# The last four units of an output projection as two blocks of Strassen's seven products, their weight sums made on GpSimd

## The chip, the cores and the metric

The kernel runs on one core of one Trainium2 chip. A core has TensorE (PE, matrix products), VectorE (DVE), ScalarE (ACT), GpSimd (POOL) and SyncE (SP), which here only issues the loads of weights. The metric is the device time of one execution in microseconds (us), the median of several runs. Everything is float32.

## The reference

One inference step of a two-layer hybrid encoder, for 256 prompt frames and 64 frames of a running stream (T = 320 frames together), 1024 channels wide. What matters here, cut:

```
h = rms(x, norm_mix);  p = h @ w_in                      # columns for four head groups of 256 channels
y_a = head_rms(lru(p), on[:G])  * gelu(lru_g)            # mixT rows 0, 1
y_b = head_rms(attention(p), on[G:2G])                   # mixT rows 2, 3
y_c = head_rms(retention(p), on[2G:3G]) * silu(r_g)      # mixT rows 4, 5
y_d = head_rms(mlstm(p), on[3G:])       * sigmoid(m_o)   # mixT rows 6, 7
x = x + concat([y_a, y_b, y_c, y_d]) @ w_out             # (320, 1024) @ (1024, 1024): the stage in question
gu = rms(x, norm_ffn) @ w_gu
x = x + (silu(gu[..., :2816]) * gu[..., 2816:]) @ w_down
```

The states of every group (latents, LRU, retention, mLSTM) are outputs too.

## The kernel before

Activations are held transposed: xT, hT and mixT are tiles of 128 channels by 320 frames, eight of each. Weights stream through a ring of five slots of 1 MB (chunks); SP loads chunk g when the use that frees chunk g-5 is done (the table LAST_USE, wait_used). Chunks o0 to o3 hold w_out, 256 output columns each, so a chunk serves two units of 128 output channels; f0 to f21 hold w_gu, then come those of w_down.

Nearly all of the large products except the output projection are already formed in blocks of Strassen's seven products: a block of two by two tiles takes seven products of half the frames (160 columns, HT) instead of eight. POOL makes three sums of the weights into spare memory and one in place (`a21 += a22`); DVE makes four sums of the activations, and puts the products together behind PE. Products 3, 5, 6 and 7 wait for POOL's sums (the semaphore "mixed"), and products 4 to 7 for those of the activations. The output projection is formed plainly: `project(n, ks)` adds the products of unit n for the tiles ks of mixT into bank n of PSUM, 320 columns each. Its order on PE follows the order in which the groups become ready: tiles 6, 7 (mLSTM), 2, 3 (attention, "mix1"), 4, 5 (retention, "mix2"), 0, 1 (LRU, "mix0"). Between them stand `pair_out` and `pair_mean` of the retention and the two mean products am0 and am1 of the LRU group, on which mix0 hangs: am0 and am1 go to ACT (two functions each), and DVE multiplies their results into mixT.

The order on each engine is written out by hand. An engine runs its instructions in that order, and `step` makes it wait for each result before the next. On POOL, the order of the stretch is: the retention states' stores, a wait until all stores have landed, the LRU stores (lru_conv, lru_h; single elements), a wait until they have landed ("a_out"), in layer 0 the loads of the next layer's latents, and then `mix_weights(l, i)` for f1, f2 and so on, the second of which waits for DVE's "h_sums". DVE waits for a_out before it makes h_sums.

Behind the projection, DVE adds each unit to xT ("x_new"), ACT squares it and multiplies it by the gain, DVE adds the squares up, PE sums them over the channels (ms2) in the middle of the first hidden units (fa0, fb0), and ACT makes rstd of that.

The part of `project` and its calls, as PE has them between the retention and the hidden units:

```
pair_mean(1, l)
project(4, (6, 7, 2, 3))
need(pe, "h_sq", l, 1)
for t in range(2):   # am0, am1
    ...
project(5, (6, 7, 2, 3))
for n in range(6):
    project(n, (4, 5))
for n in range(6):
    project(n, (0, 1))
for n in range(6, KT):
    project(n, (6, 7, 2, 3, 4, 5, 0, 1))
```

## Time and profile before

| | |
|---|---|
| three runs | 901.88, 902.30, 902.46 us; median 902.3 |
| profiled execution | 902.27 us, its span 900.40 us |
| PE, busy | 893.2 us, 99% |
| DVE, busy | 510.7 us, 57% |
| POOL, busy | 512.6 us, 57% |
| ACT, busy | 226.7 us, 25% |
| share of the chain of waits on PE | 86% |
| the output projection's line (L1295) in that chain | 7.7% |

The span runs from the first instruction to the last; the time of the execution has a little around it. A busy share is the share of the span in which the engine had an instruction under way. The chain of waits follows back from the last instruction, at each step to what released it. In timelines each row has the start in us, the duration in us, the engine, the line of the kernel, the operation, what it writes and reads, and in brackets how long the engine was idle before it and what ended that.

### The profile page before, as it was taken

How to read it: one execution, taken by the hardware profiler on the slowest of the kernel's cores; microseconds unless marked ns; L12 is line 12 of the kernel's file. 1: busy time of each engine (PE TensorE's matmuls, PEld its weight loads, DVE VectorE, ACT ScalarE, POOL GpSimd, SP SyncE). 2: the span in 40 equal slices, each digit the busy share in tenths (PEclk: the TensorE clock that was granted, in tenths of full speed). 3: DMA queues.
4: the chain of work that ended last, by engine and by line, in shares of the span. 5: the costliest groups of instructions: out<-in, count | busy, mean ns of one | idle time of the engine just before them, and what ended most of it. 6: DMA issues, size and time to landing. Idle time of an engine off the chain costs nothing.

```text
span 900.4 us, 15552 instructions
## 1 busy us (share of the span) xinstructions
PE 893.2 (99%) x5984; PEld 813.1 (90%) x5984; DVE 510.7 (57%) x1001; ACT 226.7 (25%) x497; POOL 512.6 (57%) x514
## 2 busy tenths in 40 slices
PE   8999999999999999999999999999999999999998
PEld 7997878778999999999979878877799999999998
DVE  6677857735656565522366776575565656573221
ACT  3334356531000000101133334573300000000001
POOL 6851474316866666666457344912297666666770
PEclk9999999999999999999999999999999999999999
DMA  9969321238545553333444774130844555434421
GB/s 277 279 107 110 104 92 52 54 82 240 141 141 142 140 140 129 130 129 130 128 134 144 31 151 98 48 97 5 191 138 140 140 140 141 141 130 130 151 83 36
DMA packets 159091, 112.92 MB, mean 125 GB/s; under 512 B 9829, under 2 KB 156682, under 8 KB 158890
## 3 DMA queue, kind: packets, MB, share of 16 engines
q1 hardware_dynamic: 154402, 104.44, 40.0%
q0 software_dynamic: 3984, 6.74, 7.3%
q8 instruction: 48, 0.79, 0.4%
q10 hardware_dynamic: 632, 0.75, 0.3%
q14 instruction: 25, 0.20, 0.1%
HBM read 108.33 MB, written 2.27 MB: 123 GB/s over the span
## 4 chain that ended last, share of the span: by engine, by line
PE 86%; DVE 7%; ACT 3%; DMA 1%; issue 1%; POOL 0%; SPq 0%; DVEq 0%; ACTq 0%; POOLq 0%
PE ps L1336 54%; PE ps L1295 8%; PE ps L871 7%; PE ps L905 3%; PE ps L891 2%; PE ps L1354 2%; PE ps L1005 1%; PE ps L1229 1%; PE ps L1093 1%; DMA out_s_mn<-sst 1%; DMA arena<-in_x_sample 1%; PE ps L1221 1%; PE ps L1062 1%; DVE work L2117 1%; PE ps L979 0%
## 5 line engine op out<-in xcount | busy, mean ns | idle before, releaser
L680 POOL TENSOR_TENSOR work<-ring 128x512 f32<-128x512 f32 (+1 forms) x66 | 81.8, 1240 | 153.9 <-issue 111.1
L1336 PE MATMUL ps<-mixT,ring 128*128 128x160 f32 x672 | 105.0, 299 | 0.0
L1336 PE MATMUL ps<-hT,work 128*128 128x160 f32 x672 | 98.5, 299 | 0.0
L1336 PE MATMUL ps<-hT,ring 128*128 128x160 f32 x672 | 98.1, 299 | 0.0
L1336 PEld LDWEIGHTS ps<-mixT,ring 128*128 128x128 f32 x672 | 95.8, 190 | 0.0
L1336 PEld LDWEIGHTS ps<-hT,ring 128*128 128x128 f32 x672 | 93.7, 190 | 0.3
L1336 PEld LDWEIGHTS ps<-hT,work 128*128 128x128 f32 x672 | 93.7, 190 | 0.0
L681 POOL TENSOR_TENSOR ring<-ring 128x512 f32<-128x512 f32 (+1 forms) x66 | 82.6, 1251 | 5.2
L682 POOL TENSOR_TENSOR work<-ring 128x512 f32<-128x512 f32 (+1 forms) x66 | 82.1, 1244 | 5.2
L1803 ACT ACTIVATE arena<-ps 128x160 f32<-128x160 f32 x42 | 12.8, 304 | 286.9 <-PE ps L1336 286.9
L683 POOL TENSOR_TENSOR work<-ring,work 128x512 f32<-128x512 f32 (+1 forms) x66 | 81.9, 1240 | 5.2
L871 PE MATMUL ps<-hT,ring 128*128 128x320 f32 x256 | 72.9, 437 | 0.0
L1295 PE MATMUL ps<-mixT,ring 128*128 128x320 f32 x256 | 70.4, 433 | 0.0
L2403 DVE TENSOR_TENSOR arena<-arena,ps 128x160 f32<-128x160 f32 x8 | 2.6, 322 | 118.6 <-ACT arena L1821 118.6
L1295 PEld LDWEIGHTS ps<-mixT,ring 128*128 128x128 f32 x256 | 48.5, 190 | 20.1
L871 PEld LDWEIGHTS ps<-hT,ring 128*128 128x128 f32 x256 | 47.4, 190 | 18.9 <-issue 1.0
L1336 PE MATMUL ps<-work,ring 128*128 128x160 f32 x352 | 55.6, 299 | 0.0
L1336 PE MATMUL ps<-mixT,work 128*128 128x160 f32 x336 | 52.5, 299 | 0.0
L1336 PE MATMUL ps<-arena,work 128*128 128x160 f32 x352 | 51.7, 299 | 0.0
L1336 PEld LDWEIGHTS ps<-work,ring 128*128 128x128 f32 x352 | 50.4, 190 | 0.0
L1336 PEld LDWEIGHTS ps<-arena,work 128*128 128x128 f32 x352 | 49.1, 190 | 0.0
L1336 PE MATMUL ps<-arena,ring 128*128 128x160 f32 x330 | 48.7, 299 | 0.0
(455 smaller groups left out, 1624.0 us busy)
## 6 DMA issues: line engine op xcount, KB each, us to landing
ring<-in_w_gu SPq DMA_DIRECT2D x88, 512.0 KB, 5.2
ring<-in_w_in SPq DMA_DIRECT2D x44, 512.0 KB, 6.4
ring<-in_w_down SPq DMA_DIRECT2D x32, 512.0 KB, 4.5
ring<-in_w_out SPq DMA_DIRECT2D x16, 512.0 KB, 4.6
ring<-in_w_down SPq DMA_DIRECT2D x16, 384.0 KB, 3.5
cst<-in_consts POOLq DMA_DIRECT2D x1, 1664.0 KB, 11.6
ring<-in_w_in SPq DMA_DIRECT2D x2, 640.0 KB, 5.8
arena<-r POOLq DMA_DIRECT2D x8, 160.0 KB, 18.0
```

Of the source, the lines that this page charges most:

```text
L680: step(tt(s3, a11, a21, ALU.subtract))
L681: step(tt(a21, a21, a22, ALU.add))
L682: step(tt(s2, a21, a11, ALU.subtract))
L683: step(tt(s4, a12, s2, ALU.subtract), "mixed")
L871: ins = mm(bank(use, 0, T, m), w[:, k, c:c + m], right[:, k, 0:T], start=(k == 0), stop=(k == KT - 1))
L891: ins = mm(bank(use, at * HT, HT), left, right, start=(opens and k == 0), stop=(k == KT // 2 - 1), skip_group_check=True)
L905: ins = mm(bank(use, at * HT, HT), left(k), right(k), start=(opens and k == 0), stop=(k == KT // 2 - 1), skip_group_check=True)
L1005: ins = mm(flat[a * HD:(a + 1) * HD, base:base + n], left(a), right(a), start=start, stop=stop, skip_group_check=True)
L1295: ins = mm(bank(u, 0, T), w[:, k, (n % 2) * P:(n % 2 + 1) * P], mixT[:, k, :], start=(k == 6), stop=(k == 1), skip_group_check=True)
L1336: ins = mm(bank(use, at * HT, HT), left, right(k), start=(opens and k == 0 and at == 0), stop=(closes and k == n - 1), skip_group_check=True)
L1354: return mm(bank(use, 0, T), w[:, k, q * P:(q + 1) * P], xg[:, k, :], start=(k == 0), stop=(k == KT - 1))
L1803: step(A(p1c[:, j % 2, :], bank(f"fa{j}", 0, HT), ACT.Copy), "p1_copied")
```

## The change

The units 4 to 7 (chunks o2 and o3) are no longer formed by `project` but as two blocks of seven products, `out_product`, with k running over the four pairs of tiles of mixT. Products 1, 2 and, for o2, 3 are begun early, for the tiles whose groups are ready. POOL makes the weights' sums of o2 and o3 (`out_weights`), in its order behind the retention stores and ahead of the LRU stores; `mix_weights(l, 0)` moves ahead of the wait for the LRU stores. DVE makes four sums of mixT ("mix_sums") after mix0, and puts the blocks together (`out_pair`); ACT copies the first product out of PSUM and squares units 4 to 7 in pairs. In layer 0 the loads of the latents wait for the last product of both blocks, as their memory holds sums.

```diff
@@ bank uses, per layer
-    u += [(f"o{n}", (n,)) for n in range(KT)]
-    u += [("ms2", (2,)), ("fa0", (0,)), ("fb0", (1,))]
+    u += [(f"o{n}", (n,)) for n in range(4)]
+    u += [("p2a", (4,)), ("p2c", (5,)), ("p3a", (6,)), ("p3c", (7,)), ("p2b", (0,)), ("p3b", (1,))]
+    u += [("ms2", (3,)), ("fa0", (0,)), ("fb0", (2,))]
@@ slots fall free
-LAST_USE.update({f"o{i}": f"o{2 * i + 1}" for i in range(4)})
+LAST_USE.update({f"o{i}": f"p{i}c" if i in OUTS else f"o{2 * i + 1}" for i in range(4)})
@@ POOL
+            def out_weights(l, i):
+                name = f"o{OUTS[i]}"
+                w, _ = quarters(name, l)
+                s2, s3, s4 = osum[i]
                 wait_chunk(pool, name, l)
                 a11, a12, a21, a22 = w[:, :, 0, 0, :], w[:, :, 1, 0, :], w[:, :, 0, 1, :], w[:, :, 1, 1, :]
                 tt = nc.gpsimd.tensor_tensor
+                step(tt(s3, a11, a21, ALU.subtract))
+                step(tt(a21, a21, a22, ALU.add))
+                step(tt(s2, a21, a11, ALU.subtract))
+                step(tt(s4, a12, s2, ALU.subtract), "mixed")
...
                         pool.wait_ge(sem("out_done"), 16 * nout[0])
                         now_made(pool, "state_out")
+                for i in range(len(OUTS)):
+                    out_weights(l, i)
                 need(pool, "lru_x_in", l, 1)
...
+                mix_weights(l, 0)
                 pool.wait_ge(sem("out_done"), 16 * nout[0])
                 now_made(pool, "a_out")
                 if l + 1 < DEPTH:
-                    wait_filled(pool, "kv2", l)
+                    for p in OUTS:
+                        wait_filled(pool, f"p{p}c", l)
                     load_latents(l + 1)
-                for i in range(MIXES):
+                for i in range(1, MIXES):
                     mix_weights(l, i)
@@ PE, after pair_mean(1, l); out_product waits for the weights' sums for 3, 5, 6, 7, for mix_sums for 4 to 7
-                project(4, (6, 7, 2, 3))
+                early, late, every = (3, 1), (2,), (3, 1, 2, 0)
+                out_product(2, 1, early, opens=True)
+                out_product(2, 2, early)
+                out_product(2, 3, early, opens=True)
                 need(pe, "h_sq", l, 1)
                 for t in range(2):
                     claim(pe, f"am{t}", l)
                     fill(mm(bank(f"am{t}", 0, AW), C("headmean"), an[:, t, :], start=True, stop=True), f"am{t}")
-                project(5, (6, 7, 2, 3))
-                for n in range(6):
+                for n in range(4):
                     project(n, (4, 5))
-                for n in range(6):
+                for which in (1, 2, 3):
+                    out_product(2, which, late)
+                out_product(3, 1, early + late, opens=True)
+                out_product(3, 2, early + late)
+                for n in range(4):
                     project(n, (0, 1))
-                for n in range(6, KT):
-                    project(n, (6, 7, 2, 3, 4, 5, 0, 1))
+                for which in (1, 2, 3):
+                    out_product(2, which, (0,))
+                for which in (1, 2):
+                    out_product(3, which, (0,))
+                out_product(2, 6, every, closes=True)
+                out_product(2, 5, every, opens=True)
+                out_product(2, 7, every, closes=True)
+                out_product(2, 4, every, closes=True)
+                out_product(3, 6, every, closes=True)
+                out_product(3, 5, every, opens=True)
+                out_product(3, 7, every, closes=True)
+                out_product(3, 3, every, opens=True)
+                out_product(3, 4, every, closes=True)
@@ ACT
-                squares(l, 1)
+                squares(l, 1, range(4))
+                for p in OUTS:
+                    need(act, "x_new", l, 2 * KT, 2 * p)
+                    wait_filled(act, f"p{p}a", l)
+                    step(A(pair_p1, bank(f"p{p}a", 0, HT), ACT.Copy), "p1_copied")
+                    squares(l, 1, range(2 * p, 2 * p + 2))
@@ DVE, after mix0
+                step(v.tensor_tensor(msum[0], m_at(0, 1), m_at(0, 0), ALU.subtract), "mix_sums")
+                step(v.tensor_tensor(msum[2], m_at(1, 1), msum[0], ALU.subtract), "mix_sums")
+                step(v.tensor_tensor(msum[1], m_at(1, 1), m_at(0, 1), ALU.subtract), "mix_sums")
+                step(v.tensor_tensor(msum[3], m_at(1, 0), msum[2], ALU.subtract), "mix_sums")
...
+                    need(dve, "p1_copied", l, P1S, NPAIR + OUTS.index(p) + 1)
+                    step(v.tensor_tensor(pair_u2, pair_p1, bank(a, HT, HT), ALU.add))
+                    step(v.tensor_tensor(x11, x11, pair_p1, ALU.add))
+                    step(v.tensor_tensor(x11, x11, bank(a, 2 * HT, HT), ALU.add), bank_read=(a, l))
+                    wait_filled(dve, b_, l)
...
+                    step(v.tensor_tensor(x22, x22, pair_u34[:, HT:T], ALU.add))
+                    step(v.tensor_tensor(x22, x22, bank(b_, 0, HT), ALU.add), bank_read=(b_, l))
+                    step(v.tensor_tensor(mid, mid, pair_u34, ALU.add))
+                    wait_filled(dve, c, l)
+                    step(v.tensor_tensor(mid, mid, bank(c, 0, T), ALU.add), "x_new")
+                    now_read(dve, c)
+                    now_made(dve, "x_new")
...
-                for n in range(KT):
+                for n in range(4):
                     wait_filled(dve, f"o{n}", l)
                     step(v.tensor_tensor(xT[:, n, :], xT[:, n, :], bank(f"o{n}", 0, T), ALU.add), "x_new")
                     now_read(dve, f"o{n}")
                     if n > 1:
...
+                        squares_so_far(n)
+                for p in OUTS:
+                    squares_so_far(2 * p)
+                    out_pair(p)
+                    squares_so_far(2 * p + 1)
```

## Rows read from the trace of the kernel before

**Rows 1.** The page: busy us (share) and instructions of PE; granted clock in 40 slices.
```profile
PE 893.2 (99%) x5984; PEld 813.1 (90%) x5984; DVE 510.7 (57%) x1001; ACT 226.7 (25%) x497; POOL 512.6 (57%) x514
...
PEclk9999999999999999999999999999999999999999
```
**Rows 2.** Waits of PE from 16 us on, longest first: us in total, times, longest.
```profile
PE ps L1229 <- ACT arena L1678: 0.8, 1, 0.8
```
**Rows 3.** The chain of waits, 160 to 215 us: start, us, engine, line, instructions.
```profile
174.16 2.15 PE ps L1295 x8
176.31 1.09 PE ps L1317 x4
177.40 23.69 PE ps L1295 x88
201.09 2.69 PE ps L1354 x10
```
**Rows 4.** The chain of waits in layer 1.
```profile
617.61 23.69 PE ps L1295 x88
```
**Rows 5.** The chain of waits: a block of 28 products, 160 columns.
```profile
475.23 7.61 PE ps L905 x56
```
**Rows 6.** Timeline of POOL, 155 to 222 us.
```profile
174.20 1.52 POOL L691 DMA_DIRECT2D out_p_lru_conv<-arena  x2 [1.77 <-DMA out_s_ret<-sst]
...
178.30 1.07 POOL L691 DMA_DIRECT2D out_s_lru_h<-arena  x2
196.56 0.76 POOL L698 DMA_DIRECT2D pckv<-in_cache_mla_ckv  x1 [17.19 <-DMA out_s_lru_h<-arena]
...
201.38 1.26 POOL L680 TENSOR_TENSOR work<-ring 128x512 f32<-128x512 f32 x1 [2.78 <-DMA ring<-in_w_gu]
202.72 1.40 POOL L681 TENSOR_TENSOR ring<-ring 128x512 f32<-128x512 f32 x1
```
**Rows 7.** Timeline of DVE, 155 to 222 us; 179.62 completes mix0.
```profile
173.96 0.83 DVE L2317 TENSOR_TENSOR arena<-arena 128x646 f32<-128x646 f32 x1
174.83 1.15 DVE L2319 SCALAR_TENSOR_TENSOR arena<-arena,cols 128x323 f32<-128x323 f32 x2
176.01 0.82 DVE L2322 TENSOR_TENSOR mixT<-work 128x640 f32<-128x640 f32 x1
...
179.62 0.23 DVE L2326 TENSOR_TENSOR mixT<-arena 128x64 f32<-128x64 f32 x1
...
201.20 0.49 DVE L2330 TENSOR_TENSOR xT<-xT,ps 128x320 f32<-128x320 f32 x1 [3.18 <-PE ps L1295]
```
**Rows 8.** Timelines where DVE and POOL meet; L2388's ns, shortest/median/longest.
```profile
527.60 2.02 DVE L2156 TENSOR_TENSOR arena<-arena 128x1792 f32<-128x1792 f32 x1
...
528.40 2.36 POOL L661 TENSOR_TENSOR pckv<-ring 128x512 f32<-128x512 f32 x1 [6.78 <-DMA out_s_mm<-mro]
...
201.83 1.15 DVE L2334 TENSOR_TENSOR hT<-hT 128x320 f32<-128x320 f32 x1
...
L2388 DVE TENSOR_TENSOR work<-arena,work x22: 324/1312/1318, 230.3 to 815.3; 128x160 f32<-128x160 f32 x22
```
**Rows 9.** Timeline of ACT, the last unit's square and gain.
```profile
201.78 0.47 ACT L1521 ACTIVATE hT<-xT 128x320 f32<-128x320 f32 x1 [3.24 <-DVE xT L2330]
202.28 0.56 ACT L1523 ACTIVATE work<-xT,cols 128x320 f32<-128x320 f32 x1
```
**Rows 10.** Busy time by stretch; the last columns are granted clock, DMA share, GB/s.
```profile
190.00:197.00 7.00, 7.00 (x28) 4.94 (x27) 3.45 (x8) 4.10 (x8) 0.44 (x1) 1.00 0.38 29
197.00:202.00 5.00, 5.00 (x20) 3.50 (x19) 1.53 (x4) 1.25 (x3) 2.22 (x4) 1.00 1.03 287
```
**Rows 11.** The same view at the end of the span.
```profile
895.00:900.00 5.00, 2.25 (x17) 1.74 (x15) 0.75 (x2) 0.76 (x2) 0.00 (x0) 0.97 0.23 66
```
**Rows 12.** Timeline of PE at both ends of the span.
```profile
1.07 4.99 PE L824 MATMUL ps<-work 128*128 128x128 f32 x24 [1.07 <-DVE work L1836]
...
897.23 0.44 PE L1414 MATMUL ps<-cst,xT 128*128 128x128 f32 x2 [0.41 <-DVE xT L2427]
```

More of the change, by code:

```diff
@@ L64 @@
 NPAIR = len(PAIRS)
+OUTS = (2, 3)
 MIXES = FT - 1 + 3 * NQ
-MADE = NPAIR + MIXES
-P1S = NPAIR + FT - 1 + NQ
+MADE = NPAIR + len(OUTS) + MIXES
+P1S = NPAIR + len(OUTS) + FT - 1 + NQ
 MSLOTS = 3
@@ L345, in build @@
         xgm = mixT
+        low = MSLOTS * 3 * 512 + KT * T
+        msum = [x.rearrange("p (k n) -> p k n", n=HT) for x in
+                (work[:, low:low + 4 * HT], work[:, low + 4 * HT:low + 8 * HT], work[:, low + 8 * HT:low + 12 * HT],
+                 arena[:, 2 * 326:2 * 326 + 4 * HT])]
+        pT1 = ytm_at + 640
+        osum = [[x.rearrange("p (k n) -> p k n", n=P) for x in three] for three in
+                ((pT0[:, 0:512], pT0[:, 512:1024], wkvb[:, :]),
+                 (work[:, pT1:pT1 + 512], work[:, pT1 + 512:pT1 + 1024], pckv[:, :, :].rearrange("p a n -> p (a n)")))]
         hp = mixT[:, :, :].rearrange("p k n -> p (k n)").rearrange("p (s k n) -> p s k n", s=4, k=4)
@@ L664, in pair_weights @@
                 step(tt(s4, a12, s2, ALU.subtract), "mixed")
+            def out_weights(l, i):
+                name = f"o{OUTS[i]}"
+                w, _ = quarters(name, l)
+                s2, s3, s4 = osum[i]
+                wait_chunk(pool, name, l)
+                a11, a12, a21, a22 = w[:, :, 0, 0, :], w[:, :, 1, 0, :], w[:, :, 0, 1, :], w[:, :, 1, 1, :]
+                tt = nc.gpsimd.tensor_tensor
+                step(tt(s3, a11, a21, ALU.subtract))
+                step(tt(a21, a21, a22, ALU.add))
+                step(tt(s2, a21, a11, ALU.subtract))
+                step(tt(s4, a12, s2, ALU.subtract), "mixed")
             def mix_weights(l, i):
@@ L1312, in _, with out_product @@
                 pair_mean(1, l)
-                project(4, (6, 7, 2, 3))
+                def out_product(p, which, ks, opens=False, closes=False):
+                    i = OUTS.index(p)
+                    use = f"p{p}" + {1: "a", 2: "a", 6: "a", 5: "b", 7: "b", 3: "c", 4: "c"}[which]
+                    if opens:
+                        claim(pe, use, l)
+                    wait_chunk(pe, f"o{p}", l)
+                    if which in (3, 5, 6, 7):
+                        need(pe, "mixed", l, MADE, NPAIR + i + 1)
+                    if which in (4, 5, 6, 7):
+                        need(pe, "mix_sums", l, 4)
+                    w, _ = quarters(f"o{p}", l)
+                    at = {1: 0, 2: 2, 6: 1, 5: 0, 7: 1, 3: 0, 4: 1}[which]
+                    for k in ks:
+                        need(pe, f"mix{k}", l, 1)
+                        left = {1: w[:, k, 0, 0, :], 2: w[:, k, 1, 0, :], 3: osum[i][2][:, k, :],
+                                4: w[:, k, 1, 1, :], 5: w[:, k, 0, 1, :], 6: osum[i][0][:, k, :],
+                                7: osum[i][1][:, k, :]}[which]
+                        right = {1: mixT[:, 2 * k, 0:HT], 2: mixT[:, 2 * k + 1, 0:HT], 3: mixT[:, 2 * k + 1, HT:T],
+                                 4: msum[3][:, k, :], 5: msum[0][:, k, :], 6: msum[2][:, k, :], 7: msum[1][:, k, :]}[which]
+                        ins = mm(bank(use, at * HT, HT), left, right, start=(opens and k == ks[0]), stop=(k == 0),
+                                 skip_group_check=True)
+                    if closes:
+                        fill(ins, use)
+                early, late, every = (3, 1), (2,), (3, 1, 2, 0)
+                out_product(2, 1, early, opens=True)
+                out_product(2, 2, early)
+                out_product(2, 3, early, opens=True)
                 need(pe, "h_sq", l, 1)
@@ L1330, in product @@
                     if p in (3, 5, 6, 7):
-                        need(pe, "mixed", l, MADE, NPAIR + i + 1)
+                        need(pe, "mixed", l, MADE, NPAIR + len(OUTS) + i + 1)
                     for k in range(n):
@@ L2363, in gate_up @@
                     p1 = p1c[:, j % 2, :]
-                    need(dve, "p1_copied", l, P1S, NPAIR + j)
+                    need(dve, "p1_copied", l, P1S, NPAIR + len(OUTS) + j)
                     step(v.tensor_tensor(u2, p1, bank(fa, HT, HT), ALU.add))
```

17 lines of the change are left out of this document (13 added, 4 removed).

## Prediction

> **What bounds the kernel now.** I read the busy shares first: PE is busy for 893.2 of 900.4 us [rows 1]. The list of waits on PE says the same from the other side: after the start its longest wait is 0.8 us [rows 2]. So every microsecond of product saved in the output projection can reach the end, and so can every microsecond that PE is made to wait. The chain of waits then gives the projection as an unbroken run on PE: pair_mean(1) to 174.16, four products, the two sums am0 and am1, 44 products to 201.09, then the first hidden units [rows 3]. Layer 1 repeats it 440.2 us later, with the same 23.69 us for the 44 [rows 4], so I work out layer 0 and double it. Last come the timelines of POOL, DVE and ACT around that run, for what the new steps must wait on.
>
> The profiled execution took 902.27 us: a span of 900.40 and 1.87 around it. The median of the three runs is 902.3, so the sum needs no correction.
>
> **Products, -2.0 us a layer.** A product 320 columns wide takes 23.69/44 = 0.538 us of PE [rows 3]; one of 160 columns takes 7.61/28 = 0.272 us (each is two instructions) [rows 5]. Removed are units 4 to 7, 32 x 0.538 = 17.23 us; added are 56 x 0.272 = 15.22 us. That is -2.01 us a layer and -4.0 us in all, the most that this change can bring.
>
> **The wait for the sums of o2, +5.5 us a layer.** After pair_mean(1) the new order on PE is products 1 and 2 of o2 for k = 3 and 1, four at 0.272 us, so at 174.16 + 1.09 = 175.25 it stands at product 3, which needs s4, the last of the four sums of o2 on POOL. These sums stand behind POOL's wait for the retention stores, in program order: POOL has issued the last of them at 172.43 and goes on only when it has landed, 1.77 us later, at about 174.15 [rows 6]. Ahead of these stores POOL mostly waits too, but the sums are queued behind and can't use it. A sum of 128x512 takes 1.27 us and the next begins 1.34 after it (201.38, 202.72 in layer 0) [rows 6], so s4 would be there at 174.15 + 3 x 1.34 + 1.27 = 179.5, and PE would wait 4.25 us. That is the lower bound.
>
> DVE disturbs them. From 173.96 to 176.83 it has four operations whose two operands are both in SBUF (646, 323, 323 and 640 columns) [rows 7], and where such operations meet POOL's the two take turns. A POOL sum that began at 528.40 during a DVE operation that ended at 529.62 ended at 530.76, 1.14 us after it; one that began at 202.72 ended at 204.12, 1.14 us after DVE's end at 202.98 [rows 6, 8]. In turn DVE's 160-column additions take 1.31 us beside POOL's (the median; the shortest, 0.32) [rows 8]. In turns, from 173.96 on: DVE to 174.79, POOL to 175.93, DVE to 176.27, POOL to 177.41, DVE to 177.75, POOL to 178.89, DVE to 179.56, POOL to 180.70 (DVE's own part is its columns at 0.96 a ns: at 202.64 POOL ended and DVE 0.34 us later for 320 columns). PE goes on at about 180.8 and has waited 5.5 us. I take 5.5, with 4.25 as the lower end and 6 as the upper.
>
> What is queued behind this wait on PE is am0 and am1. ACT and DVE then make mix0 of them: 3.54 us from the start of am0 to mix0 now [rows 3, 7]. am0 would start at 181.3, and with the sums of o3 on POOL beside DVE's four multiplications mix0 comes at about 186.7. PE asks for it after am (182.4), eight products of units 0 to 3 on mixT 4 and 5 (4.3) and nine small ones (2.4), at 189.2: covered by 2.5 us. It is covered now by 6.2 us (186.0 against 179.85). The four new mix_sums on DVE, 0.82 us each as the multiplication of the same 640 columns [rows 7], end at 190.2; PE wants them at 194.9. The sums of o3 end at 186.2 and are wanted later still. Without the wait, PE would be through with the projection at 199.1; with it, at 204.6.
>
> **Behind the projection, +1.0 us a layer.** Now one addition (0.49), a square and a gain on ACT (0.47, 0.56) and an addition (0.49) stand between the last unit and ms2, and PE covers them with five products (2.69 us) [rows 3, 7, 9]. In the new order units 6 and 7 are finished together, ACT's copy of p1 for o3 stands behind the squares and gains of units 4 and 5, and DVE does eight additions per pair. Counted from p2c (5.4 us ahead of the end): 0.6 for x_new, 2.1 for ACT's four, 0.3 for the copy, 2.8 for seven additions, 0.5 for the last, then square 6 and the addition to hT, about 1.1, plus four hand-overs of 0.1: the sum of squares is ready some 2.9 to 3.0 us after the end of the projection, not 2.69. That is +0.3 with POOL idle. But POOL forms the sums of f1 in this stretch, and four of these additions read SBUF alone; each pays up to 0.98 us [rows 8].
>
> When f1 arrives is open. Its slot falls free with unit 1, 20 products behind am (177.40 + 10.8 = 188.2), and POOL starts on it at 201.38; the transfers move only 29 GB/s from 190 to 197 and 287 after that, and the LRU stores, issued from 174.20 to 179.4, are waited for until 196.56 [rows 6, 10]. The new order issues these stores at 186.2 to 191.4 and f1 at 191.5, so if the stores hold the loads, f1 comes at 208 to 211; if not, at about 197. Early, it collides with the additions above. Late, its sums collide with h_ready (four operations of 640 columns, 0.82 us each alone), and a_out, which now also waits for these sums, comes at 214 to 217, where DVE wants it from about 213. In both cases I get 0.3 to 2.5 us and take 1.0. The latents are loaded later, after p3c; they are needed only at the end of the layer.
>
> **The clock, +1.3 us a layer.** The granted clock is full in every slice of the page [rows 1], with PE never idle for long; the last stretch, in which PE's last instruction starts at 897.23 and takes 0.44, shows 0.97: it fell to the lower level (1.2 GHz from 2.4) within the 2.8 us left [rows 11, 12]. A wait of 5.5 us is longer than anything that PE sees now, so I expect a fall in it. The first 24 instructions of the warm-up, 128 columns, take 4.99 us, 0.208 each [rows 12], where 160 columns take 0.136 later [rows 5]: half the speed. So a spell at the lower level lasted some 5 us here and would cost 2.5 us. The bounds are 0 and 2.5; part of a spell passes within the wait, so I take 1.3.
>
> The Trainium skill ("TensorE: Matmul & The Clock Gate", "What's actually happening") says that the throttled state is the default and activity releases it, so an idle array falls back. That a fall happens in mid-kernel no run here shows. By this rule the term stays; without it the sum would end 2.6 us lower.
>
> Another of its pages ("Perfetto Trace Analysis", the notes on GpSimd's profile boundary) has it that POOL's shown spans are unreliable and should be taken from start to start. With 1.27 us a sum the wait would be 0.3 us shorter than with the 1.34 that I took from the starts.
>
> **The sum.** -2.0 + 5.5 + 1.0 + 1.3 = +5.8 us a layer, +11.6 in all: 902.3 + 11.6 = 913.9 us.
>
> **Rivals.**
> *The clock holds.* The wait is there but PE stays at the upper level. For it: no fall is seen between the start and the end. 902.3 + 2 x 4.5 = 911.3 us.
> *No turns between POOL and DVE.* DVE's operations leave POOL alone; the wait is 4.25 us, the slip 0.3, the clock costs little (0 to 1): 902.3 + 2 x (-2.0 + 4.25 + 0.3 + 0.3) = 908.0 us. Against it stand the pairs of rows above.
> *f1 late.* The stores hold the loads longer than now; product 3 of f1 waits for POOL, and a_out holds the h_sums: 1.5 to 3 us a layer more, 917 to 920 us.
> *The sums are in time: faster.* If s4 of o2 is there when PE asks, only -2.0 and +0.3 a layer remain: 898.9 us. It decides at 177.0: s4 must come by then for the layer to be no slower, that is, POOL must start at 171.6 at the latest. What would allow it is that the wait for the stores isn't what holds POOL from 172.43 to 174.20. The trace names the landing of out_s_ret as releaser [rows 6], and even a start at 172.43 is too late.
> *Nothing changes*: only if gain and wait happened to cancel, s4 at 177.0.
>
> **Chances.** Forecast, with a fall of the clock in at least one layer: 0.50. Clock holds: 0.22. No turns: 0.08. f1 late: 0.12. In time: 0.06. Cancel: 0.02. A measurement of this kernel can tell about 0.2% (1.8 us) from no change; hence faster 0.06, same 0.02, slower 0.92. The range: the low ends of wait and slip without the clock give 908, the high ends with it 919; I set 908.5 to 918.0, which leaves out the fastest cases and part of f1 late.
>
> **What would show it.** PE idle ahead of the third product of o2 in both layers, released by POOL's fourth sum: 5.5 us (right), under 2 us (the wait was wrong). POOL's four sums spread over 6.5 us, not 5.4 (the turns). A granted clock under 1.00 in the 10 us behind the wait, with 160-column products at about 0.54 us. 56 products in 15.2 us. mix0 never waited for. Five products of f0 and then a gap of 0.3 to 2.5 us ahead of ms2, or a gap in f1. The prediction is wrong if POOL's sums of o2 start ahead of the retention stores, or if PE's wait is there but filled by work that the order lets pass.

## The result

The changed kernel takes 924.75 us (median of four runs, 923.31 to 926.25), the kernel before 902.38 (901.88 to 902.80): a ratio of 1.0247, 95% interval 1.0235 to 1.0259, so 22.4 us slower. The forecast was +11.6 us, with a range that ended at 918.0: the direction was right, the size half of what came, and the time lies outside the range.

The profiled execution took 926.25 us, its span 924.4. The page, to be laid beside [rows 1]: busy us of the engines, and the granted clock in 40 slices.

```profile
PE 900.9 (97%) x6080; PEld 826.4 (89%) x6080; DVE 538.3 (58%) x1033; ACT 228.0 (25%) x501; POOL 536.2 (58%) x530
...
PEclk9999999898999999999999999998999999999999
```

PE is busy 7.7 us longer than before, though the new order holds 4 us less of products, and its clock is no longer full in three slices. The rest is waiting. The waits of PE from 16 us on, where before had none over 0.8 us [rows 2] (us in total, times, longest):

```profile
PE ps L1359 <- POOL wkvb L687: 9.6, 2, 4.8
PE ps L1359 <- issue: 3.4, 1, 3.4
PE ps L1418 <- DVE hT L2409: 3.3, 2, 2.1
PE ps L1404 <- DVE hT L2444: 1.2, 1, 1.2
```

The first is product 3 of o2 waiting for POOL's s4, in both layers; the second a pause put down to no releaser, in layer 0; the third the sum of the squares (ms2); the fourth a product of f1, in layer 1. The timeline of PE has them in order, layer 0 (the line of [rows 3] in which the 44 products ran without a gap):

```profile
173.58 1.25 PE L1359 MATMUL ps<-mixT,ring 128*128 128x160 f32 x8
179.63 1.40 PE L1359 MATMUL ps<-mixT,wkvb 128*128 128x160 f32 x4 [4.80 <-POOL wkvb L687]
180.83 2.36 PE L1371 MATMUL ps<-arena,cst 128*128 128x323 f32 x4
182.98 4.96 PE L1322 MATMUL ps<-mixT,ring 128*128 128x320 f32 x16
...
201.32 0.98 PE L1359 MATMUL ps<-work,ring 128*128 128x160 f32 x6
205.66 1.09 PE L1359 MATMUL ps<-work,ring 128*128 128x160 f32 x2 [3.36 <-issue]
206.54 2.34 PE L1359 MATMUL ps<-work 128*128 128x160 f32 x8
...
217.12 1.65 PE L1418 MATMUL ps<-hT,cst 128*128 128x320 f32 x4 [2.15 <-DVE hT L2409]
218.57 7.54 PE L1422 MATMUL ps<-work,ring 128*128 128x320 f32 x22
```

Layer 1 has the first wait again, and a longer stretch of slow rows behind it:

```profile
635.22 1.40 PE L1359 MATMUL ps<-mixT,wkvb 128*128 128x160 f32 x4 [4.80 <-POOL wkvb L687]
636.42 2.36 PE L1371 MATMUL ps<-arena,cst 128*128 128x323 f32 x4
638.58 5.84 PE L1322 MATMUL ps<-mixT,ring 128*128 128x320 f32 x16
```

The timeline of the kernel before has this for am0 and am1:

```profile
176.15 1.25 PE L1317 MATMUL ps<-arena,cst 128*128 128x323 f32 x4
```

Four 323-column instructions (am0, am1) take 2.36 us behind the first wait and 1.25 in the kernel before; eight of 160 columns take 1.25 at 173.58 and 2.34 at 206.54. That is the lower clock. The same stretches by window (the last three columns are granted clock, DMA share, GB/s):

```profile
175.00:183.00 8.00, 3.37 (x9) 2.59 (x10) 4.95 (x4) 1.16 (x3) 7.61 (x6) 0.63 0.01 2
...
197.00:204.00 7.00, 5.30 (x39) 5.05 (x38) 0.96 (x3) 0.30 (x1) 0.00 (x0) 1.00 0.45 31
204.00:211.00 7.00, 5.31 (x19) 5.18 (x20) 3.10 (x7) 2.24 (x5) 0.00 (x0) 0.53 0.66 118
211.00:217.00 6.00, 3.98 (x19) 2.83 (x17) 4.93 (x9) 1.02 (x3) 4.26 (x4) 0.98 1.14 303
217.00:221.00 4.00, 3.88 (x9) 2.54 (x10) 1.03 (x3) 3.25 (x6) 3.27 (x4) 0.64 1.20 293
```

The clock fell three times in layer 0 (in the wait for s4, in the pause, and 1.0 us after the wait for ms2) and once in layer 1, in the wait for s4. The DMA row at 197 to 204 moves 31 GB/s where before had 287 from 197 to 202 [rows 10]. POOL's timeline shows what moved with it:

```profile
173.35 1.27 POOL L684 TENSOR_TENSOR arena<-ring 128x512 f32<-128x512 f32 x1 [1.35 <-DMA out_s_ret<-sst]
174.70 1.73 POOL L685 TENSOR_TENSOR ring<-ring 128x512 f32<-128x512 f32 x1
...
177.98 1.39 POOL L687 TENSOR_TENSOR wkvb<-ring,arena 128x512 f32<-128x512 f32 x1
...
185.38 1.55 POOL L714 DMA_DIRECT2D out_p_lru_conv<-arena  x2 [0.29 <-POOL pckv L687]
...
212.50 1.26 POOL L703 TENSOR_TENSOR work<-ring 128x512 f32<-128x512 f32 x1 [21.89 <-DMA ring<-in_w_gu]
```

The LRU stores go out 11.2 us later than in [rows 6] (185.38 against 174.20), and f1 is there 11.1 us later (212.50 against 201.38). DVE has a pause of its own in this stretch, between two additions of the first block; its operand from PE was complete at 199.3:

```profile
206.28 0.49 DVE L2421 TENSOR_TENSOR pair_t<-ps,pair_t 128x320 f32<-128x320 f32 x1 [7.59 <-remote]
```

The profiled executions differ by 926.25 - 902.27 = 24.0 us. The four falls of the clock, each the slow rows less the same groups at the full clock (1.25 us for four instructions of 323 columns, 4.47 for sixteen of 320, 0.71 for four of 160), cost 2.3, 3.1 and 1.9 us in layer 0 and 3.2 in layer 1, together 10.4 (or 10.6 by PE's busy time, 900.9 us against 890.3 in e7_tail_reordered below, which has the same 6080 instructions and in its profile a clock that never fell). Products -4.0, wait for s4 +9.6, the pause +3.4, the waits for ms2 and for h_ready +4.5 and the clock +10.4 make +23.9. That it closes so well is partly an offset of two errors of about 1 us: by busy time the seven products gave back only 2.9 us (890.3 against 893.2), and PE's idle time grew by 16.3 us (23.5 against 7.2), not by the 17.5 of these waits.

### The profile page after: what moved, and what is told of

It reads as the page before. It is cut to its first block, busy times and chain, and to the rows that moved or that the text cites. A ratio compares the mean times of both kernels' runs of the same rounds, so it can differ in the third digit from the quotient of the medians.

```text
span 924.4 us, 15855 instructions
## 1 busy us (share of the span) xinstructions
PE 900.9 (97%) x6080; PEld 826.4 (89%) x6080; DVE 538.3 (58%) x1033; ACT 228.0 (25%) x501; POOL 536.2 (58%) x530
## 4 chain that ended last, share of the span: by engine, by line
PE 82%; DVE 7%; ACT 4%; DMA 2%; POOL 2%; issue 2%; another core or an unknown queue 1%; SPq 0%; DVEq 0%; ACTq 0%; POOLq 0%
PE ps L1404 52%; PE ps L932 7%; PE ps L898 6%; PE ps L918 2%; PE ps L1322 2%; PE ps L1120 1%; PE ps L1359 1%; PE ps L1089 1%; PE ps L1152 1%; PE ps L1422 1%; DVE hT L2444 1%; DMA out_s_mn<-sst 1%; PE ps L1248 1%; DMA arena<-in_x_sample 1%
## 5 line engine op out<-in xcount | busy, mean ns | idle before, releaser
L1404 PEld LDWEIGHTS ps<-mixT,ring 128*128 128x128 f32 x672 | 95.8, 190 | 0.0
L1404 PEld LDWEIGHTS ps<-mixT,work 128*128 128x128 f32 x336 | 47.9, 190 | 0.0
L1404 PEld LDWEIGHTS ps<-arena,ring 128*128 128x128 f32 x330 | 46.1, 190 | 0.0
```

The costliest lines, as they stand in the source:

```text
L1404: ins = mm(bank(use, at * HT, HT), left, right(k), start=(opens and k == 0 and at == 0), stop=(closes and k == n - 1), skip_group_check=True)
```

## The experiments

All were timed beside the kernel before (901.7 to 902.1 us in the five groups of runs). Each time is a median, each ratio one to the kernel before on the same chip, with its 95% interval.

### e1_third_product_last: the wait for the sums taken away

```diff
-                out_product(2, 3, early, opens=True)
...
-                for which in (1, 2, 3):
+                for which in (1, 2):
...
+                out_product(2, 3, every, opens=True)
                 out_product(2, 4, every, closes=True)
```

> The changed kernel with one move on PE: product 3 of o2 is formed as a whole right ahead of its product 4 instead of early, so nothing on PE asks for POOL's sums before 190 us. Theory S (the wait for s4 of o2 and the clock that it costs are nearly all of the loss; the rest follows it): -2.0 us of products and +0.3 a layer remain, 899 us. Theory W (the LRU stores, issued at 185 to 191 instead of 174 to 179, hold all DMA until 17 us after the last one, so loads and instruction fetches come late): the wait of 4.8 us goes, but f1 still lands at about 212 and PE then waits for its sums for about 7 us a layer, with a fall of the clock: 914 to 920 us.

Measured: 920.4 us (914.1 to 921.1), ratio 1.019 (1.0157 to 1.0224). The wait for s4 is gone and only 4.4 us with it (the profiled execution, at 914.1 us, is 6 us quicker than the other three, so its trace shows the mildest case). The time is about what theory W said; its mechanism, some 7 us a layer of waiting for f1's sums, isn't there (1.2 us in all). Something else took the place of the wait for s4, on PE:

```profile
PE ps L1322 <- DVE mixT L2395: 6.8, 2, 4.3
```

and on DVE, which makes mix2 between POOL's sums:

```profile
174.37 2.04 DVE L2392 SCALAR_TENSOR_TENSOR arena<-arena,cols 128x323 f32<-128x323 f32 x2
176.44 1.77 DVE L2395 TENSOR_TENSOR mixT<-work 128x640 f32<-128x640 f32 x1
```

In [rows 7] the same two lines take 1.15 and 0.82 us and end at 176.83. With POOL's sums beside them they end at 178.21, and product 3 no longer stands ahead as work for PE. The sums at this place cost a wait either way: for themselves, or for what they hold up.

The Trainium skill ("SBUF — State Buffer", "Who interferes with whom") says that a DVE instruction with both inputs in SBUF contends with a GpSimd instruction that reads SBUF, and that one with at most one SBUF input, outside the two-port modes, doesn't. The traces agree on both halves: 1.77 against 0.82 us here, while the addition that reads PSUM (L2428 of the changed kernel, at 215.50 us) takes 0.49 us beside POOL's sums as without them.

### e2_no_lru_stores: the changed kernel without the LRU stores

Its edit leaves the eight `out(...)` calls of lru_conv and lru_h in each layer out, so these states aren't written.

> The changed kernel without the stores of the LRU states (lru_conv and lru_h of both layers are left out of the outputs); all else as changed. Theory W: f1 lands at about 200 in layer 0, the pause of PE in the middle of a product (3.4 us) and of DVE (7.6 us) go; the wait for s4 (4.8) with its clock (about 3.3) stays: 915 to 918 us. Theory S: the late stores are no cause, 924 to 925 us.

Measured: 918.2 us (914.7 to 919.1), ratio 1.0185 (1.0168 to 1.0202), 6.6 us less than the changed kernel and about what theory W gave. The pause of PE and that of DVE are gone, the two waits of 4.8 us for s4 stand. The DMA queues from 182 to 209 us, first of the changed kernel, in which not one block of the queue "instruction" falls in these 27 us:

```profile
DMA packets 1283, 0.53 MB, mean 20 GB/s; under 512 B 264, under 2 KB 1283, under 8 KB 1283
...
q1 hardware_dynamic: 1027, 0.52, 22.2%
q0 software_dynamic: 256, 0.01, 1.9%
```

and then of e2:

```profile
DMA packets 7661, 3.89 MB, mean 144 GB/s; under 512 B 112, under 2 KB 7659, under 8 KB 7659
...
q8 instruction: 1, 0.02, 0.3%
q14 instruction: 1, 0.01, 0.1%
```

The 256 small packets of q0 are the LRU stores, 8 KB by the sizes of their eight issues. In the changed kernel the loads of weights on q1, issued from 192.57, move at most 72 GB/s in any microsecond up to 206, and 251 or more only from 209; in e2 they run at 220 to 346 GB/s from 193.5 to 200. So the stores slow them. But the recorded packets of q0 all lie between 186 and 192, before the slow stretch; what holds the queues after that, the trace doesn't show.

### e3_before_late_stores: only the stores late, in the kernel before

```diff
+                wait_filled(pool, "o0", l)
                 need(pool, "lru_x_in", l, 1)
```

> The kernel before, with one wait added on POOL: the LRU stores are issued when unit 0 of the projection is done (about 187.2 us in layer 0), 13 us later than before and 2 us later than in the changed kernel. No Strassen in the projection, no sums. Theory W: the stores hold f1 until about 210; f1's sums end at about 219 and PE waits for them about 6 us a layer, plus the clock and perhaps a pause for instructions: 918 to 926 us. Theory S or any theory in which the late stores only delay a_out (which would come at about 209.6, ahead of DVE's need at 210.2): 902 to 903 us.

Measured: 929.5 us (928.6 to 931.7), ratio 1.031 (1.0295 to 1.0326): with no other edit, stores that go out 13 us later cost 27.8 us, more than theory W gave them. POOL's row:

```profile
214.50 0.76 POOL L698 DMA_DIRECT2D pckv<-in_cache_mla_ckv  x1 [22.22 <-DMA out_s_lru_h<-arena]
```

and PE's waits:

```profile
PE ps L1337 <- issue: 17.7, 2, 9.4
PE ps L1337 <- DMA ring<-in_w_gu: 3.4, 2, 2.9
```

The stores land 22.2 us after the last was issued (24.4 in layer 1), where before it was 17.2 [rows 6], and PE waits for the load of f1 itself. But the 9.4 us are no pause: PE goes on at 222.88, 0.1 us after POOL's fourth sum of f1 has ended (221.52 + 1.26). In this order the sums of f1 stand behind the wait for the landing, so the wait put down to "issue" is one for POOL. The experiment shows that late stores are dear. It doesn't show that this is the price they have in the changed kernel, where f1's sums stand ahead of that wait; the nearest figure for that is e2's 6.6 us.

### e4_wait_filled: the wait for s4 filled with products

```diff
+                claim(pe, "am0", l)
+                for _ in range(9):
+                    mm(bank("am0", 0, T), chunk("o2", l, 256)[:, 6, 0:P], mixT[:, 6, :], start=True, stop=True)
                 out_product(2, 3, early, opens=True)
```

The nine products are of no use to the result; they only keep PE at work.

> The changed kernel with nine useless products of 320 columns (4.84 us, into the bank of am0, results unused) on PE ahead of product 3 of o2, where PE waits 4.8 us. If the waiting itself is the whole price, the time stays at 924 to 925 us. If the fall of the granted clock in it is a price of its own (2.4 us in layer 0 and 3.3 in layer 1 by the profile), the time falls to about 919 us, and the granted clock is full until the tail of the projection in both layers.

Measured: 915.1 us (914.9 to 915.6), ratio 1.0148 (1.0133 to 1.0163). PE can go on no earlier than in the changed kernel (179.43 us against 179.63), yet the kernel is 9.6 us faster, and its clock is 1.000 on the mean of the span in all four runs. In the profiled execution PE's busy time without the useless products (18 x 0.538 = 9.7 us) is 891.5 us, 9.4 less than in the changed kernel: that is the clock. PE's other idle time is 2.0 us less: the pause of 3.36 us isn't there, although the stores go out as late (185.21), and smaller waits grew. The forecast had 2.6 for the clock.

### e5_stores_first: the stores back in their place

The edit takes e1 and puts `out_weights` for o2 and o3 behind the LRU stores, `mix_weights(l, 0)` back behind the wait for their landing.

> The change, with POOL's order of before around the stores (LRU stores, then the sums for o2 and o3, then the wait until the stores have landed, then the sums for f1) and product 3 of the first block formed late, whole, ahead of product 4, as in e1_third_product_last. Theory A (stores that are issued late hold the loads of the weights and PE's own instructions): the stores end by about 179.5 us as before the change, POOL starts on f1 at about 196.5, no pause of PE put down to issue and none of DVE put down to another core; the sums for o2 are ready about 6 us later than in the changed kernel (185 to 187), ahead of product 3; time = before 901.7 minus 4.0 for the products plus 0 to 2 behind the projection, 897.7 to 901. Theory B (the cost is the sums themselves, in turns with DVE at the shared port, and the blocks' additions on DVE, wherever the stores stand): mix2 and mix0 late by 3 us or more, time 908 to 916.

Measured: 909.6 us (905.8 to 910.1), ratio 1.0072 (1.0049 to 1.0094), 10.8 us less than e1, which has late stores and the same order on PE. Two things differ between them, the stores and the place of POOL's sums, and with the sums the wait for mix2 shrank too, from 6.8 to 1.3 us; the 10.8 us aren't the price of the stores alone. Theory A is right on what it removes: PE has no pause, and the windows show 259 GB/s from 197 to 204. POOL starts on f1 at 202.35 us, near the 201.38 of before and not at the 196.5 of the expectation. The time isn't 898 to 901. What is left is mainly one wait, for the sum of the squares, and the fall of the clock behind it in layer 0. PE's waits:

```profile
PE ps L1417 <- DVE hT L2408: 7.1, 2, 4.6
PE ps L1321 <- DVE mixT L2394: 1.3, 2, 0.6
```

The chain of waits names what stands between the last product (ended at 199.5) and ms2: start, us, what.

```profile
199.39 0.48 ACT hT L1588
...
199.89 0.57 ACT work L1590
...
200.49 0.31 ACT pair_t L1860
...
202.50 1.33 DVE xT L2423
...
204.21 1.12 DVE xT L2425
...
205.35 0.50 DVE xT L2427
...
206.44 0.50 DVE hT L2408
...
206.98 2.50 PE ps L1417 x4
```

ACT still squares units of the first block when the second is ready, then copies p1, then DVE puts the block together, two of its additions in turns with POOL (1.33 and 1.12 for 0.33 and 0.50), and only then come the last squares. ms2 comes 7.5 us behind the last product, in layer 1 5.3, where before has 2.7 [rows 3]. With what layer 0 has more goes a pause of DVE, put down to nothing on this core, and there although the stores are in their old place:

```profile
195.95 0.49 DVE L2420 TENSOR_TENSOR pair_t<-ps,pair_t 128x320 f32<-128x320 f32 x1 [2.71 <-remote]
```

### e6_sums_in_idle: the sums for o2 15 us earlier

```diff
+                        wait_filled(pool, "bo1", l)
+                        out_weights(l, 0)
```

ahead of the states' stores of that group; PE's order is the changed kernel's, the LRU stores stand where they did before.

> The change, PE's order untouched (product 3 of the first block ahead of am0 and am1), but POOL makes the sums for o2 in its idle stretch some 15 us earlier (behind bo1, ahead of the states' stores of that group), the LRU stores stand where they stood in the kernel before, the sums for o3 follow them, and the sums for f1 all come behind the wait for the stores. Theory A: no wait of PE for the sums, no fall of the clock in the stretch, no pause put down to issue, f1 begun at about 196.5 us: 897.7 to 901. Theory B: four sums beside DVE's work at 147 to 161 us slow DVE there by 3 to 4 us in each layer, and the waits for it show on PE: 905 to 912.

Measured: 914.1 us (912.6 to 915.8), ratio 1.0135 (1.012 to 1.015). The time is a little above theory B's. There is no wait for s4, but DVE's work beside the sums ends later and PE waits for it ahead of the projection (1.4 and 0.7 us, 2.1 in each layer), and the same wait stands behind the projection (4.6 and 2.7 us). Two operations of 323 columns took 1.70 us there (L2325, 152.36) for 0.81 in the kernel before. An engine's idle time isn't free if its work slows another engine.

### e7_tail_reordered: e5 with the queue behind the projection mended

```diff
@@ DVE
+                squares_so_far(4)
                 for p in OUTS:
-                    squares_so_far(2 * p)
                     out_pair(p)
-                    squares_so_far(2 * p + 1)
+                for n in (5, 6, 7):
+                    squares_so_far(n)
@@ ACT
                     step(A(pair_p1, bank(f"p{p}a", 0, HT), ACT.Copy), "p1_copied")
+                for p in OUTS:
                     squares(l, 1, range(2 * p, 2 * p + 2))
```

> e5_stores_first with one more edit behind the projection: ACT copies product 1 of the second block (o3) before it squares the units of the first, and DVE puts both blocks together before it adds up the squares. In e5 PE waited 4.65 and 2.44 us there for the sum of the squares, and its clock fell behind the longer wait. Theory C (the two last units of a block end together and the queue ACT squares, ACT copy, DVE block, ACT squares, DVE sum stands behind the last product: 5.4 us where the kernel before has 1.9): both waits go to 0 to 1 us, no fall of the clock, PE reaches the hidden units 4 to 7 us earlier over both layers: 899 to 903, from e5's 909.6. Theory D (the wait in layer 0 is DVE's pause, put down to a remote cause at 193 to 196, and not the queue): only layer 1's 2.4 us goes: 906 to 908.

Measured: 903.4 us (902.8 to 905.7, 11 runs), ratio 1.0024 (1.0015 to 1.0033): just above theory C. 6.2 us went with an edit that touches only the order on ACT and DVE. Both waits shrank to 1.7 us, not to the 0 to 1 that C had, and the clock held for the whole span of the profiled execution (903.3 us). Three of the eleven runs took 905.5 to 905.7 us at a mean clock of 0.997 to 0.998. The pause of DVE in layer 0 was 1.15 us here, for 2.71 in e5, so a part of what layer 0 gained may be that.

### e8_idle_and_tail and e9_change_and_tail: the same edit on e6 and on the change

> e6_sums_in_idle with the same edit behind the projection. Theory C: 914.1 minus 7 to 9, 904 to 907 (what stays over e7 is the 2 us in each layer that the sums for o2 take from DVE ahead of the retention's products). Theory D: 910 to 912.

Measured: 910.0 us (905.2 to 912.3), ratio 1.0084 (1.0059 to 1.0109), between the two theories: 4 us went, one of the two waits stayed at 3.2 us.

> The changed kernel itself with only that edit behind the projection. Its waits there were 2.15 and 1.13 us, and behind the first its clock fell once more. Theory C: 924.7 minus 3 to 5, 920 to 922, since the wait for the sums, the late stores and their pauses stay. Theory D: 923 to 925.

Measured: 923.1 us (922.3 to 925.5), ratio 1.024 (1.0226 to 1.0254): only 1.6 us less than the change, the two intervals overlap, and the time is theory D's. Behind the late stores the mended tail has nothing to show: PE's pause (3.17 us) and DVE's (7.22) are there again, at the same place, and the waits for ms2 make 3.8 us for 3.3. The tail is a second cause that shows when the first is gone.

### e10_sums_interleaved and e11_product_moved_up: two attempts at the last 1.6 us

e10 puts `squares_so_far(5)` and `(6)` ahead of the last addition of the second block. e11 is e10 with half of product 1 of o3 ahead of am0 and am1:

```diff
+                out_product(3, 1, early, opens=True)
                 need(pe, "h_sq", l, 1)
...
-                out_product(3, 1, early + late, opens=True)
+                out_product(3, 1, late)
```

> e7_tail_reordered with DVE adding the squares of units 4 and 5 ahead of its last addition of the second block instead of behind it. In e7 three additions (3.5 us) stood between that last addition and PE's sum, and PE waited 1.70 and 1.65 us. Theory C (the queue behind the last product sets the end): the waits shrink to 0.3 to 0.7 us each, 900.7 to 901.5, against e7's 903.4 and before's 901.8. If the last addition itself slips by what is put ahead of it (0.7 us or more, in turns with POOL), the waits stay above 1 us: 902.5 to 903.5.

Measured: 906.1 us (902.8 to 906.9), ratio 1.0036 (1.0022 to 1.0049), slower than e7 by the median, though the intervals overlap. In layer 1 the two additions met POOL's sums of f1 and took 2.91 us, the block's last addition slipped with them, PE waited 3.25 us and its clock fell.

> e10_sums_interleaved with half of product 1 of o3 (tiles 6, 7 and 2, 3) formed ahead of am0 and am1, which takes bank 5 in place of 6 for am0. It puts 1.1 us of PE's work ahead of mix2, for which PE waited 0.65 us in each layer in e5 and e7 since product 3 was moved away. Theory: both waits go, 1.3 us less than e10: 899.4 to 900.2, so faster than before by 0.2% or a little more. If mix0, which hangs on am0 and am1, then comes too late for the tiles 0, 1 (it has 3 us to spare), the time is that of e10 or more.

Measured: 906.5 us (905.4 to 908.1), ratio 1.0046 (1.0033 to 1.0059). The wait for mix2 (1.0 us over both layers in e10) is gone as expected, and the wait for ms2 grew from 5.0 to 5.7 in all. Both expectations missed: they counted positions in a queue and not who reads SBUF meanwhile.

### e12_only_h_late: fewer late stores

e3 without the four lru_conv stores of each layer (that state isn't written).

> e3_before_late_stores (the kernel before, LRU stores held back until o0 is filled; 27.8 us slower) without the four lru_conv stores of each layer: only the four lru_h stores go out, late (it leaves out the LRU convolution state). Theory A1 (the hold is the time the queue takes for the single elements of all stores, and lru_conv carries three of every four): the hold is a quarter, the stores land about 5 us after their issue and the time is 902 to 906. Theory A2 (any such store issued then holds the loads for some 17 to 22 us, whatever its size): 915 to 930.

Measured: 910.5 us (909.3 to 911.9), ratio 1.009 (1.0077 to 1.0103), neither A1's time nor A2's. The price is 8.3 us, not 27.8. But the length of the hold is A2's; POOL goes on only here:

```profile
207.75 0.77 POOL L698 DMA_DIRECT2D pckv<-in_cache_mla_ckv  x1 [18.17 <-DMA out_s_lru_h<-arena]
```

A quarter of the elements still lands 18.2 us after its issue, against 22.2 for all. So the hold is 4 us shorter for three quarters less, and it ends 6.8 us earlier (207.75 against 214.50), 2.7 of them because the last issue is earlier. That the price follows from when it ends, and what is due then, is argued from this one pair. Why a few elements hold the queues so long, these runs don't tell.

### e13_pe_sums_squares and e14_product_up_tail: place or port

Both are e7 with the half product moved up. In e13, moreover, PE adds the squares of units 5, 6 and 7 itself:

```diff
+                    squares_sum(5, 1)
+                    squares_sum(6, 2)
-                    fill(squares_sum(KT - 1, 1), "ms2")
+                    fill(squares_sum(KT - 1, 3), "ms2")
...
-                for n in (5, 6, 7):
-                    squares_so_far(n)
+                squares_so_far(5)
```

> e7_tail_reordered with the half product moved up as in e11, and with PE adding the squares of units 5, 6 and 7 itself (four products of 0.4 us instead of two), so that DVE has one addition (unit 4's) behind its last block instead of three. Theory E (what is left of the wait is DVE's additions in SBUF taking turns with POOL's sums for f1 or its loads of latents: 3.4 to 3.5 us for three that take 0.49 us each): the wait for DVE's sum goes to 0 to 0.5 us, 0.8 us of products come in for each layer, and the mix2 wait is gone: 903.4 - 1.3 - 3.3 + 1.6 = 900.4 (899.5 to 901.5). If ACT's squares are what comes last (square 7 ends at 202.0 in e7, 1.6 us behind the last addition), 901 to 902.

> e7_tail_reordered with the half product moved up and nothing else: 903.4 - 1.3 = 902.1 if the mix2 wait of 0.65 us in each layer goes and nothing takes its place; 903.0 or more if what comes after (mix0, the sums of mixT, the additions behind the last product) is moved into POOL's sums instead, as e11 seemed to show (906.5 against e10's 906.1).

Measured: e14 907.1 us (906.5 to 908.0), ratio 1.0055 (1.0041 to 1.007); e13 901.5 us (900.9 to 903.6, 11 runs), ratio 0.9997 (0.9988 to 1.0006). The two differ by two additions of 320 columns in each layer, which DVE makes behind its last block in e14 and PE in e13, and by 5.6 us. In e14 DVE's three additions there took, shortest, median, longest in ns (layer 0):

```profile
L2410 DVE TENSOR_TENSOR hT<-hT x3: 493/1434/2304, 200.8 to 203.7; 128x320 f32<-128x320 f32 x3
```

Three take 1.5 us with POOL idle, 4.3 here. PE waited 3.18 us for them in layer 0 and 2.77 in layer 1, and the clock fell behind the longer one. e13 has no wait in layer 0 (chain of waits; to be read beside [rows 3]):

```profile
195.88 2.99 PE ps L1358 x22
198.87 2.69 PE ps L1422 x10
201.57 2.15 PE ps L1418 x8
```

It is the best of these versions with seven products, and it only equals the kernel before: of the 2.0 us saved in a layer, PE's two further sums take 1.08 back (2.15 for eight instructions, 1.08 for four before), and what is left over both layers, 1.8 us less a wait of 0.9 in layer 1, is about what the measurement can tell.

## Why the prediction was right and wrong

The time of 913.9 us was too low by 10.9, and the step that failed most is the term for the clock: one fall a layer at 1.3 us, where the trace has four falls at 1.9 to 3.2 us. A pause of PE and the waits behind the projection, which the sum had at nothing and at half, do the rest. Terms for both layers, us:

| term | forecast | measured in the profile |
|---|---|---|
| products | -4.0 | -4.0 by their starts, -2.9 by PE's busy time |
| wait for s4 | +11.0 | +9.6 |
| behind the projection | +2.0 | +4.5 |
| the clock | +2.6 | +10.4 |
| pause of PE | none | +3.4 |

That the direction was right owes little to luck: the wait for s4 alone is more than the products give. The wait came out 1.4 us under the forecast, so the terms that were too small are short by more than the total shows.

**What bounds the kernel**: right. PE's waits and its clock account for the 24.0 us to about 1 us.

**Products, -2.0 us a layer**: right. In the changed kernel a product of four k (eight instructions) starts every 1.09 us, 0.272 for each pair.

**The wait for the sums of o2, +5.5**: right in cause and nearly in size, 4.80 us in both layers, inside its bounds of 4.25 and 6. POOL began when out_s_ret had landed, as said, and its four sums took 6.0 us (173.35 to 179.37), between the 5.3 without turns and the 6.55 of the turns written out; three of the four were lengthened (1.73, 1.40, 1.39). mix0 and mix_sums were in time, as said. e1 adds what the forecast hadn't: without this wait, one for mix2 stands in its place.

**Behind the projection, +1.0**: it measured 2.15 in layer 0 and 1.13 + 1.23 in layer 1, within its bounds (0.3 to 2.5) with some luck. The step of it that failed is the count from p2c. As written its terms add up to 7.8 us, 2.4 behind the end of the projection and not 2.9 to 3.0, so it gave no slip at all with POOL idle. It assumed that DVE puts the first block together 0.6 us after p2c; in e5, layer 1, the block ended 2.0 us after it, because DVE had begun late, and the second block's additions took 4.4 us, not 2.8, in turns with POOL. In e5 that makes waits of 4.65 us (with DVE's pause) and 2.44, where the term was 1.0; the changed kernel hides a part of it behind its other losses.

**The clock, +1.3**: right that it falls, wrong by a factor of four in what it costs: 10.4 us by the rows, 9.4 by e4, where 2.6 were in the sum. The spell was sized from the kernel's start at 5 us. Here the first one of each layer lasts 6.8 us (177.1 to 184.0 in layer 0), and how much of it passes within the wait, for which the text had no row, isn't fixed: 2.5 us in layer 0, 0.7 in layer 1, and the price is 2.3 us in the one and 3.2 in the other. So the upper bound of 2.5 a layer was too low even for a single fall, and a second fall behind a second wait wasn't thought of. The terms' high ends, moreover, add up to 920.3 us and not 919, and the range was cut to 918.0; the measured time lies above both. In e7, whose two waits there are 1.7 us, the clock held in the profiled execution.

The Trainium skill ("TensorE: Matmul & The Clock Gate", "What's actually happening") has the throttled state as the default that activity lifts, and the trace agrees now in mid-kernel too: 0.53 from 204 to 211 us, in the pause and behind it.

**The stores**: this is the term that wasn't in the sum. The text had its premise, that stores issued at 186 to 191 might hold the loads and bring f1 at 208 to 211 (it was 212.5), but asked only who waits for f1 and made a rival of it, 917 to 920 us with a chance of 0.12. Missed was that the engines themselves may stand: PE stands for 3.36 us in the middle of a product whose operands are all there, DVE for 7.59 us between two additions, and behind PE's pause the clock falls once more (3.1 us). Leaving the stores out (e2) is worth 6.6 us, and both pauses are gone.

What the pauses wait for stays open. That they are a want of instructions is a conjecture. For it: they go with the stores in e2 and come again in e9, PE's lies inside a product, and no instruction block is recorded from 182 to 209 us. Against it: the next blocks are recorded at 210 and 212 us, when PE (205.66) and DVE (206.28) have gone on; e1 and e4 go over 35 us without a block on q8, with stores as late (186.76 and 185.21), and PE has no such pause; and DVE has shorter ones (1.15 us in e7, 2.71 in e5) with the stores in their old place. So late stores alone don't bring PE's pause, and no run took the engine's supply apart from the loads. The Trainium skill ("Runtime: NRT & Kernel Launch", "Instruction fetch mechanics") describes such blocks, fetched ahead over a DMA queue of the engine's own, and calls the cost mostly hidden; whether a fetch stood behind the 3.36 us of PE, no run here shows.

**Rivals.** "The clock holds" (911.3) fell with the first window at 0.63. "No turns" (908.0) is out by the 6.0 us. "f1 late" was the nearest in time and right that the stores hold the loads, but its price, 3 to 6 us, was to come from product 3 of f1 waiting for POOL, and the trace has no such wait. "In time" needed a POOL that starts by 171.6; it started at 173.35. What e13 shows of that rival: with no wait for sums, the best version tried brings 0.4 us, which can't be told from nothing, and not the 3.4 that were written for it, because of the tail.

## What to carry to other kernels

When work is put ahead of a store or a load on a queue, the transfer's whole slow stretch moves with it: look up how long it holds the other queues and lay that window over what will then be due. Price a wait on TensorE together with the clock behind it, and allow for a fall with each wait of the lengths seen here, from 2.15 us on (1.9 to 3.2 us of PE each). Sums handed to GpSimd cost the VectorE operations with two SBUF inputs that run beside them, and a block that finishes several units at once needs its queue behind the last product written anew, which was worth more here (6.2 us) than the products it saved.

## What was not expected of the hardware

- Behind eight stores of single elements (8 KB in all) the loads of weights ran at 31 GB/s from 197 to 204 us and at 303 from 211 to 217, though the stores' own packets are recorded before 192; the landing, where a wait for it shows it, came 17 to 24 us after the last issue, and 18 for a quarter of the elements.
- DVE's addition of 320 columns with both inputs in SBUF took up to 2.46 us beside POOL (e7) for 0.49 alone.
- Three falls of the clock within 41 us of one layer, each for 3.4 to 6.9 us, with idle stretches of 4.80, 3.36 and 2.15 us. The length of the wait alone doesn't decide: the clock fell with 2.15 (changed kernel) and 2.65 us (e6, layer 1) and held with 2.44 (e5) and 2.77 (e14).
- A wait put down to "issue" can be one for an engine that finished just before: in e3 it was POOL's sum, 0.1 us earlier.
